# Second attention of a two-block model: the compressed values of one head in each of a pair's two jobs

## The reference: what is computed

```python
o_c = jnp.einsum('bqghn,bngd->bqghd', p_c.astype(v_cmp.dtype), v_cmp)     # 31 compressed keys
o_s = jnp.einsum('bqghk,bqgkd->bqghd', p_s.astype(vs.dtype), vs)          # selected blocks
o_w = jnp.einsum('bqghk,bkgd->bqghd', p_w.astype(vw.dtype), vw)           # window
o = gt[..., 0:1] * o_c + gt[..., 1:2] * o_s + gt[..., 2:3] * o_w
```

## Time and profile before

| What | Value |
|---|---|
| time, median of 3 runs | 1934.17 us (1933.32 to 1936.07) |
| the profiled execution: its own time | 1936.29 us |
| its span, first to last instruction | 1934.5 us |
| TensorE busy | 1891.3 us, 98% |
| VectorE, ScalarE, GpSimd busy | 983.0, 761.2, 763.3 us |
| mean granted TensorE clock | 0.987 |
| chain that ended last | TensorE 89%, VectorE 6%, ScalarE 4% |

### The profile page before, as it was taken

The page is one execution under the profiler, slowest core; times in us unless marked ns, Lnnn a source line. Parts: engine busy times, 40 slices in busy tenths (PEclk is TensorE's granted clock), DMA queues, the critical chain, the costliest instruction groups (busy, mean ns, idle before and its releaser), DMA issues.

```text
span 1934.5 us, 25284 instructions
## 1 busy us (share of the span) xinstructions
PE 1891.3 (98%) x9354; PEld 1545.6 (80%) x9354; DVE 983.0 (51%) x1639; ACT 761.2 (39%) x1307; POOL 763.3 (39%) x325
## 2 busy tenths in 40 slices
PE   7988999999999999999999999999999999999998
PEld 6886688888888788888888888898866688888886
DVE  6767367643344544235444333743688444344444
ACT  6786544322223351233222222423599642222221
POOL 4323043543444334454445444356300135445452
PEclk9998999999999899999999999999999999999999
DMA  5212032332323223973323333234112023323321
GB/s 190 66 45 66 19 102 69 114 105 87 103 86 103 67 83 108 164 194 100 99 97 97 106 101 95 79 100 136 39 34 67 21 80 118 98 87 97 98 91 62
DMA packets 52238, 177.55 MB, mean 92 GB/s; under 512 B 5527, under 2 KB 5911, under 8 KB 52152
## 3 DMA queue, kind: packets, MB, share of 16 engines
q1 hardware_dynamic: 47952, 166.22, 27.1%
q10 hardware_dynamic: 4200, 10.15, 3.5%
HBM read 166.88 MB, written 9.47 MB: 91 GB/s over the span
## 4 chain that ended last, share of the span: by engine, by line
PE 89%; DVE 6%; ACT 4%; issue 1%; DMA 0%; ACTq 0%; DVEq 0%
PE ps L422 27%; PE ps L423 27%; PE ps L424 27%; PE ps L907 2%; ACT arena L1112 2%; PE ps L893 1%; DVE arena L2263 1%; DVE arena L2240 1%; PE ps L930 1%; DVE arena L1651 1%; ACT arena L1069 1%; PE ps L608 1%; PE ps L574 1%; PE ps L579 1%; PE ps L592 1%
## 5 line engine op out<-in xcount | busy, mean ns | idle before, releaser
L383 POOL TENSOR_TENSOR WL<-raw,WH 128x1024 fp32r<-128x1024 f32 x295 | 736.2, 2510 | 1103.6 <-ACT WH L994 1103.4
L422 PE MATMUL ps<-XH,WH 128*128 128x512 f32 (+1 forms) x1280 | 497.5, 389 | 10.6 <-DMA ident<-in_ident 10.6
L994 ACT ACTIVATE WH<-raw 128x1024 fp32r<-128x1024 f32 x295 | 304.4, 1053 | 509.6 <-PE ps L424 461.0
L423 PE MATMUL ps<-XL,WH 128*128 128x512 f32 (+1 forms) x1280 | 495.8, 387 | 0.0
L424 PE MATMUL ps<-XH,WL 128*128 128x512 f32 (+1 forms) x1280 | 495.6, 387 | 0.0
L422 PE MATMUL ps<-HH,WH 128*128 128x512 f32 x1080 | 423.6, 392 | 5.3 <-DVE XL L1784 4.5
L424 PE MATMUL ps<-HH,WL 128*128 128x512 f32 x1080 | 421.4, 390 | 0.0
L423 PE MATMUL ps<-HL,WH 128*128 128x512 f32 x1080 | 421.2, 390 | 0.0
L422 PEld LDWEIGHTS ps<-XH,WH 128*128 128x128 f32 x1280 | 243.0, 190 | 59.6 <-issue 11.4
L424 PEld LDWEIGHTS ps<-XH,WL 128*128 128x128 f32 x1280 | 242.8, 190 | 48.0
L423 PEld LDWEIGHTS ps<-XL,WH 128*128 128x128 f32 x1280 | 243.0, 190 | 47.2
(11 more groups left out here) (260 smaller groups left out, 1715.0 us busy)
## 6 DMA issues: line engine op xcount, KB each, us to landing
raw<-in_weights SPq DMA_DIRECT2D x301, 512.0 KB, 3.6
tab<-arena ACTq DMA_DIRECT2D x1, 5120.0 KB, 76.7
arena<-tab SPq DMA_DIRECT2D x16, 256.0 KB, 2.9
ftab<-arena ACTq DMA_DIRECT2D x1, 2080.0 KB, 23.4
h<-in_xT SPq DMA_DIRECT2D x8, 256.0 KB, 8.8
out_T<-h SPq DMA_DIRECT2D x8, 256.0 KB, 2.1
arena<-ftab ACTq DMA_DIRECT2D x4, 256.0 KB
arena<-in_pT ACTq DMA_DIRECT2D x1, 512.0 KB, 3.5
```

The source lines that it names most:

```text
L383: nc.gpsimd.tensor_tensor(WL[:, s, :], raw[:, s, :], WH[:, s, :].bitcast(f32), SUB)\
L422: nc.tensor.matmul(out, wh, xh, start=start, stop=False)
L423: nc.tensor.matmul(out, wh, xl, start=False, stop=False)
L994: nc.scalar.activation(WH[:, s, :], raw[:, s, :], ACT.Copy).then_inc(*m["whi"].tick())
```

## The change

The compressed values of head 0 are multiplied in the pair's branch-0 job, those of head 1 in its branch-1 job. In a branch-0 job the matmul of head 0 now starts the accumulation of the lower 64 partitions; the upper 64 are started by head 1's first value matmul. The order of the two heads within a block of keys is turned in branch-0 jobs (head 1 first), so that the two halves of the array's columns alternate from the first matmul on.

```diff
-                if job.br == 0:
-                    if job.pair:
-                        pe.wait_ge(sems["pv_out"], job.pair)
-                    for r in range(2):
-                        i = job.heads[r] % HG
-                        nc.tensor.matmul(out[r], VC[32 * i:32 * i + 32, HD * job.g:HD * job.g + HD],
-                                         PCT[32 * i:32 * i + 32, job.g, :], start=True, stop=False, skip_group_check=True)
+                if job.br == 0 and job.pair:
+                    pe.wait_ge(sems["pv_out"], job.pair)
+                i = job.heads[job.br] % HG
+                nc.tensor.matmul(out[job.br], VC[32 * i:32 * i + 32, HD * job.g:HD * job.g + HD],
+                                 PCT[32 * i:32 * i + 32, job.g, :], start=job.br == 0, stop=False, skip_group_check=True)
...
-                        for r in range(2):
+                        for r in (1 - job.br, job.br):
                             last = nc.tensor.matmul(out[r][:, kt * P:S], job.value(kt), PT2[r][:, at:at + S - kt * P],
-                                                    start=False, stop=job.br == 1 and (g, kt) == (2, 2), skip_group_check=True)
+                                                    start=(job.br, r, kt) == (0, 1, 0), stop=job.br == 1 and (g, kt) == (2, 2),
+                                                    skip_group_check=True)
```

## The result

The changed kernel takes 1937.56 us as median of 20 runs, against 1933.91 us of the kernel before in 20 runs: ratio 1.0018, 95% interval 1.0011 to 1.0025. It is slower by 3.7 us, between 2.1 and 4.8 by the interval. The forecast was 4.3 us slower, 1938.5 us.

A forecast was written before the change was run, and what follows sets the result against it. TensorE was taken to bound even places, VectorE odd ones. Five odd places (+2.1 us), places 3 and 5 (+1.2) and place 17 (+1.0) gave +4.3 us on 1934.17, so 1938.5 us; range 1934.0 to 1941.5.

The forecast's parts named there:

- TensorE bounds the even places, VectorE the odd ones: Places are successive attention jobs on TensorE's timeline: place 8 takes 8.26 us, place 9 7.84 us with 0.58 us slack at most.
- A compressed matmul alone costs 1.00 us: At each job's compressed matmul: the two heads' matmuls run together, so one alone costs the pair's full 1.00 us.
- It finds no partner, because of the shape: The other half's first value matmul has 128 rows, not 32, so it cannot overlap the compressed one; even places gain nothing.
- 5 x 0.42: Places 7, 9, 11, 13 and 15 go from 7.84 to 8.26 us, +0.42 us each, +2.1 us.
- 2 x 0.60: Places 3 and 5 lose their waits on ScalarE's copy and take +0.60 us each, +1.2 us.
- 1.0: Place 17, among projections and without a wait, pays the whole +1.0 us.
- Halves in turns: Rival: the array's column halves take turns, so a lone compressed matmul costs 0.5 us; sum -2.7 us, 1931.5 us; 8%.
- Overlap with the other half's value matmul: Rival: compressed matmul overlaps the other half's first value matmul; even places gain about 0.15 us; sum +1.9 us, 1936.1 us; 20%.
- ScalarE behind: Rival: ScalarE's later eviction makes six even places' compressed matmuls wait, 0.3 us each; +6.1 us in all, 1940.3 us; 12%.

The follow-up runs named there:

- kernel with padded rows: Changed kernel with each head's compressed values on 128 rows, zeros outside its 32, same head order; 1935.97 us, ratio 1.0017 to the kernel before.
- padded kernel before: Kernel before, both heads still in the branch-0 job, with compressed values on 128 rows, zeros outside a head's 32; 1933.83 us, ratio 0.9996.

## Why the prediction was right

*TensorE bounds the even places, VectorE the odd ones.* Right. The changed kernel has 8.27 and 8.26 us where the sum had 8.26 for both, the wait on line 2263 is gone, and the kernel with the pair in the odd place turns the pattern over.

*A compressed matmul alone costs 1.00 us.* Right: 0.48 us between its passes and 0.99 to 1.00 us to the values. The pace of the transposes, one stream on the whole array, was the row that told it: two records that start together and take one stream's time are two streams at once.

*It finds no partner, because of the shape.* Right, but with some luck: it was the choice with the least behind it, one gap of 0.06 us. The kernel with padded rows shows it: same order, same shape, and the two start together. The Trainium skill's rule in TensorEngine Tiling (Array Packing), Key Properties, that changing the tiling mode drains TensorE, agrees with this pair of runs. The size of the gap was wrong. The padded kernel before puts the change at 0.14 us, 0.09 of it at that gap. The pace of 0.115 us for 128 columns took in the slower first step of the ten transposes (0.17 us); the others follow by 0.11 us, so 512 columns need 0.44 us and not 0.46.

*The sum.* 5 x 0.42 + 2 x 0.60 + 1.0 = 4.3 us was expected in the attention, 4.1 measured. Counted from first value matmul to first value matmul, the step from place 2 to 3 has 1.00 us more and that from 3 to 4 0.41 less, so place 3 costs 0.59 us where 0.60 was forecast; place 5 costs 0.57 us, place 17 0.99 us, and places 7 to 13 0.41 to 0.43 us each. The one term that was off is place 15, which cost 0.26 us, not 0.42. Before the change it held a second wait that its four like do not have. Behind its transposes stands a projection that waits for VectorE's last logits. These ended at 1520.62 and the projection began at 1520.68, 0.18 us behind the last transpose's start; in the changed kernel it is 0.03 us. So place 15 had more slack to fill. The medians moved by 3.7 us, with 4.1 well inside the interval.

*The rivals.* Halves in turns: refuted by the passes 0.48 us apart (it needed under 0.3). Overlap with the other half's value matmul: refuted for the changed kernel by the 1.00 us lead, in either order of the heads. In the padded kernel, where it does happen, the attention is 1.7 us longer than before; the rival's price was +1.9. ScalarE behind: its copy, exponentials and eviction came later as worked out, but the eviction started 0.72 us ahead of the matmul that needs it, and no wait appeared. The rival had put the need at 0.64 us, so it was close. The Trainium skill's Gotcha 1 in TensorEngine Tiling (Array Packing), that tiles in different rows cannot use one PSUM bank at once, does not show here: in the kernel before the two compressed matmuls lie in different rows, write different partitions of bank 6, and cost together what one costs alone.

*The chances.* "Slower by over 0.2%" had 0.52, "the same" 0.44. The measured 0.18% lies just below that bound and its interval, 0.11 to 0.25%, on both sides of it, so the runs do not decide between the two. That the kernel became slower at all is clear of the noise.

## What to carry to other kernels

Before sharing work out among two stages, ask what it ran beside. Two matmuls in separate halves of the array's columns that run together cost what one does; split up, each costs the full price, unless its new neighbour in the other half has the same shape (shown by the padded kernel) and the halves stay equally long (worked out from their columns, not tried). To halve such a pair between two stages, cut its columns and keep the pair. To see how much slack a change filled, compare busy time and time over the same stretch: here 7.2 and 4.1 us in the attention. The busy time of the whole page, 9.7 us more, also took in 2.5 us from elsewhere.

## What was not expected

- When the even places lose their compressed matmuls, TensorE's slack does not open where the odd places had it. The larger part, 0.44 to 0.49 us, is a wait for ScalarE's copies ahead of the value matmuls, and only 0.19 us stays on VectorE. The place still takes 7.87 to 7.89 us.
- The scatter of whole runs, some 7 us between the fastest and the slowest, is not seen in the attention. From the first to the last value matmul it was 134.0 and 134.1 us in the changed kernel and the one with the old order, while the start lay anywhere from 1403.5 to 1410.9 us in the nine profiles, mostly with the same program ahead of it. Why the start moves was not tried.
- Multiplying by 96 rows of zeros costs no time that the runs show, and takes away a change of shape that costs 0.14 us.
